# Weighted sums of a head pair gathered in one PSUM bank and read once, in the three attention stages of a two-block transformer

## The chip, the cores and the metric

One core of one Trainium2 chip runs the whole program; nothing is shared with other cores. The metric is the time of one execution on the device in microseconds (us). The engines are TensorE (PE, with its weight loads as PEld), VectorE (DVE), ScalarE (ACT), GpSimd (POOL) and SyncE (SP, which issues the transfers). Each works through its own list of instructions in order, and they meet only at semaphores. PSUM, which TensorE writes, has eight banks of 512 floats on each of the 128 partitions; they are numbered 0 to 7 below.

## The reference, cut to what matters

The input has 512 tokens of width 1024. Two blocks follow one another, each of two layers. Three of the layers hold attention with 16 heads of dimension 64, and these three are what the change touches:

```python
# first block, odd layer: keys chosen by top_k of an index score, bias by distance
logits = einsum('bqhd,bqkhd->bqhk', qb, ksel) * C_HEAD_DIM ** -0.5 + bias
probs  = softmax(where(valid, logits, -inf))
out    = einsum('bqhk,bqkhd->bqhd', probs, vsel)
return x + (out * silu(z)) @ w_out

# second block, layer 0: window of 128 keys, one sink per head
o = banded_attention(q, k, v, A_WINDOW, rel_table, sinks)
return o.reshape(B, S, ATTN_WIDTH) @ w_o + b_o

# second block, layer 1: three branches, each with its gate
o = gates[..., 0:1] * o_cmp + gates[..., 1:2] * o_slc + gates[..., 2:3] * o_win
return o.reshape(B, S, ATTN_WIDTH) @ w_o
```

The rest is dense projections, a chunkwise recurrence, pooling, norms and two feed-forward layers.

## The kernel before, in words

The program is a list of stages, and each stage hands every engine its own code. The order of the work on an engine is written out by hand in loops over steps; no scheduler moves anything.

Class `Attention` (line 1906) is used three times: for the odd layer of the first block (below: the first attention stage), for the windowed layer (the second) and for the two full branches of the last layer (the third; its compressed branch is computed before and lies in `oT`). The work is cut into steps `(m, t, e)`: `m` is one of 8 pairs of heads (128 features), `t` one of 4 query tiles of 128 queries, `e` the branch. In a pair, the tiles come in the order 3, 1, 2, 0, so the number of 128-key blocks in a causal step goes 4, 2, 3, 1. The first and second stage have 4 steps per pair (`per_pair`) and 32 in all (`NS`); the third has two branches, 8 steps per pair and 64 in all.

A step `s` goes through a pipeline:

- PE `score(s)`: the products of queries and keys into two of the banks 0 to 3 (L2002; in the first stage two matmuls with the mask stand ahead of some, L1999).
- DVE `logit(s)`: adds the bias, writes the logits to SBUF and keeps the row maximum (L2070). ACT `exp(s)` follows (L2164), then DVE `share` (the reciprocal of the row sum, L2076) and POOL `divide` (L2128).
- PE `turn(s)`: transposes of the probabilities, 2 per key block (L2016), into banks 4 and 5 for even steps or bank 6 for odd ones. DVE and ACT `keep(s)` copy them to SBUF (L2098, L2100, L2173).
- PE `mix(s)`: probabilities times values, 2 matmuls per key block (L2033), one for each head of the pair, into the upper or lower 64 partitions of a piece 128 columns wide, which method `O(s)` names.
- DVE `finish(s)`: reads that piece, 128 partitions x 128 columns, and adds it to `oT` (third stage, L2086), multiplies it into `zT` (first stage, L2088) or copies it to `oT` (second stage, L2090), and counts up `att_outs`.
- When the steps of a pair are done, ACT `split_high(m)` (L2177) and POOL `split_low(m)` (L2140) make the two parts of the pair's rows that the following projection multiplies.

Round `s` of the PE loop issues `score(s)`, `turn(s-3)`, `mix(s-5)`. Round `s` of the DVE loop issues `finish(s-6)`, `logit(s)`, `share(s-1)`, `keep(s-3)`. ACT's `split_high` stands in round 6 after the last step of a pair, POOL's `split_low` in round 7 after it.

Where a step can have more than two key blocks (first and third stage, flag `halves`), all pieces lie in columns 0 to 127 of bank 7, so each `mix` waits until the `finish` of the step before it has read them; only the last three steps alternate between banks 3 and 7. In the second stage the pieces alternate between banks 7 and 5, and a `mix` waits for the `finish` of the step two before it. After the last `score`, in round `NS`, the PE code also runs `lead_in`, the first products of the following projection (L298 to L300: 6 of the 8 blocks of its first tile, three matmuls each); after the last `mix` that projection goes on with its second tile.

Of the kernel before, what the change touches and what calls it, by code (L numbers as in the profile page):

```python
# [24 lines left out]
ALU = mybir.AluOpType  # L25
# [3 lines left out]
P = 128  # L29
SEQ = 512  # L30
DM = 1024
MT = DM // P
# [1873 lines left out]
class Attention(Stage):  # L1906
# [5 lines left out]
    def __init__(self, k, q, key, value, keys, n_bias, out, hi, lo, room, before=None, table=None, bias=None, add=False, times=None,  # L1912
                 mask=None, sink=None, gate=None, branches=1, bias_all=None, masked_bias=None, ready=None, finishing=None,
                 mask_made=None, turning=None, first_pe=None, first_act=None, trail_act=None, first_dve=None):


        self.k, self.q, self.key, self.value, self.keys, self.n_bias = k, q, key, value, keys, n_bias
        self.out, self.hi, self.lo, self.before, self.table, self.bias = out, hi, lo, before, table, bias
        self.add, self.times, self.mask, self.sink, self.gate = add, times, mask, sink, gate
        self.bias_all, self.masked_bias, self.ready_q, self.finishing, self.mask_made = bias_all, masked_bias, ready, finishing, mask_made  # L1920
        self.trail, self.trail_act = before is not None and before.trail is not None, trail_act
        self.turning, self.first_pe, self.first_act, self.following = turning, first_pe, first_act, None
        self.first_dve = first_dve
        self.pad = 0 if sink is None else 1
        self.pooled = (1, 2) if masked_bias is not None else ()
        self.steps = [(m, t, e) for m in range(MT) for e in range(branches) for t in (3, 1, 2, 0)]
        self.NS, self.per_pair = len(self.steps), 4 * branches
        probs_of, self.pT, self.st = room
        self.probs_of = [ap.rearrange("p (x n) -> p x n", x=2) for ap in probs_of]
        self.turned_of = [self.pT[:, 0:1024], self.pT[:, 1024:1536]]  # L1930
        self.T = [k.banks[:, 4:6, :].rearrange("p a b -> p (a b)"), k.banks[:, 6, :]]
        self.flip = 1 if before is not None and before.bank(before.last_in_turn()) < 2 else 0
        NS, sg = self.NS, k.sig
        self.landed = [sg(f"att_bias{i}").take(16 * (MT // 2) if bias is not None else 0) for i in range(2)]
        self.scores, self.logits = sg("att_scores").take(NS), sg("att_logits").take(2 * NS)
        self.probs, self.dens = sg("att_probs").take(2 * NS), sg("att_dens").take(NS)
        self.ready, self.turned, self.mixed = sg("att_ready").take(2 * NS), sg("att_turned").take(NS), sg("att_mixed").take(NS)
        self.kept = [sg(n).take(NS // 2) for n in ("att_kept_even", "att_kept_odd")]
        self.halves = len(keys(3)[2]) > 2
        self.rest = sg("att_kept_rest").take(NS // 2 if self.halves else 0)  # L1940
        self.outs = sg("att_outs").take(NS)
        self.added = sg("att_bias_masked").take(2 * MT if self.pooled else 0)
        self.high, self.low = sg("att_high").take(MT), sg("att_low").take(MT)

# [5 lines left out]

    def O(self, s):

        if not self.halves:
            return self.k.banks[:, 7 - 2 * (s % 2), 0:P]
        return self.k.banks[:, 3 if s in (self.NS - 3, self.NS - 1) else 7, 0:P]

    def with_mask(self, m, t):
        to = self.masked_bias[:, m % 2, 0:2, :] if t == 1 else self.masked_bias[:, m % 2, 2:5, :]
# [23 lines left out]
    def on_pe(self, pe):  # L1982
        nc, before, evac = self.k.nc, self.before, self.k.sig("tile_steps")
        steps, keys, S, T, kept = self.steps, self.keys, self.S, self.T, self.kept
# [36 lines left out]
        def mix(s):  # L2021
            m, t, e = steps[s]
            blocks = keys(t)[2]
            if s == self.NS - 3 and self.halves:
                pe.wait_ge(self.logits.sem, self.logits.at(2 * self.NS))
            pe.wait_ge(self.outs.sem, self.outs.at(s if s < self.NS - 3 and self.halves else s - 1))
            pe.wait_ge(kept[s % 2].sem, kept[s % 2].at(s // 2 + 1))
            if self.halves and s % 2 == 0:
                pe.wait_ge(self.rest.sem, self.rest.at(s // 2 + 1))
            last = len(blocks) - 1  # L2030
            for b, (kb, r) in enumerate(blocks):
                for x in range(2):
                    ins = nc.tensor.matmul(self.O(s)[64 * x:64 * x + 64, :], self.value(e, m, x, kb, r),  # L2033
                                           self.turned_of[s % 2][0:r, (2 * b + x) * P:(2 * b + x + 1) * P],
                                           start=(b == 0), stop=(b == last))
            ins.then_inc(self.mixed.sem, 1)

        for s in range(self.NS + self.MIX):
# [14 lines left out]
    def on_dve(self, dve):  # L2053
        nc, steps, keys, st, pad = self.k.nc, self.steps, self.keys, self.st, self.pad
# [20 lines left out]
            dve.wait_ge(self.probs.sem, self.probs.at((s + 1) * 2))  # L2075
            nc.vector.reciprocal(st[:, s % 4, 2, :], st[:, s % 4, 1, :]).then_inc(self.dens.sem, 1)  # L2076

        def finish(s):
            m, t, e = steps[s]
            r = slice(t * P, (t + 1) * P)  # L2080
            o = self.out(m)[:, r]
            dve.wait_ge(self.mixed.sem, self.mixed.at(s + 1))
            if self.finishing is not None and s % self.per_pair == 0:
                self.finishing(dve, m)
            if self.add:
                nc.vector.tensor_tensor(o, self.O(s), o, ALU.add).then_inc(self.outs.sem, 1)  # L2086
            elif self.times is not None:
                nc.vector.tensor_tensor(o, self.O(s), self.times(m)[:, r], ALU.mult).then_inc(self.outs.sem, 1)  # L2088
            else:
                nc.vector.tensor_copy(o, self.O(s)).then_inc(self.outs.sem, 1)  # L2090

        def keep(s):
            blocks = keys(steps[s][1])[2]
# [6 lines left out]
                nc.vector.tensor_copy(self.turned_of[0][0:r, 512:w], self.T[0][0:r, 512:w]).then_inc(self.rest.sem, 1)  # L2100

        for s in range(self.NS + self.FINISH):
            if 0 <= s - self.FINISH < self.NS:
                finish(s - self.FINISH)
            if s < self.NS:
                logit(s)
            if 0 <= s - 1 < self.NS and not (self.trail and s == 2):
                share(s - 1)
            if self.first_dve is not None and s < 2:
                self.first_dve(dve, s)  # L2110
            if self.trail and s == 1:
                share(1)
            if self.trail and s == 2:
                self.before.evict(dve, "dve", self.before.tiles - 1)
            if 0 <= s - self.TURN < self.NS and (self.halves or (s - self.TURN) % 2 == 1):
                keep(s - self.TURN)
# [39 lines left out]
    def on_act(self, act):  # L2156
# [16 lines left out]
            nc.scalar.activation(self.turned_of[0][0:r, 0:w], self.T[0][0:r, 0:w], ACT.Copy).then_inc(self.kept[0].sem, 1)  # L2173

        def split_high(m):
            act.wait_ge(self.outs.sem, self.outs.at(self.per_pair * (m + 1)))
            nc.scalar.activation(self.hi(m), self.out(m), ACT.Copy).then_inc(self.high.sem, 1)  # L2177

        for s in range(self.NS + self.HIGH):
# [967 lines left out]
```

## Time and profile before

| | |
|---|---|
| time, median of 3 runs | 1933.11 us (1933.01 to 1933.32) |
| profiled execution, first to last instruction | 1933.0 us |
| PE busy | 1910.9 us, 99% of the span |
| DVE busy | 1056.5 us, 55% |
| ACT busy | 769.1 us, 40% |
| POOL busy | 353.2 us, 18% |
| chain that ended last: share of PE | 90% |
| chain: share of DVE | 6% |

The span of the profile is 0.1 us from the median, so a sum made against the profiled execution can be set against the median as it stands. The chain is followed back from the last instruction, at each step to what released it. An engine's idle time ahead of an instruction is given with the instruction that ended it; where the profile says "issue", the engine waited for nothing that it shows. The ends of matmuls are modelled, and the starts are measured: how long a group of matmuls really took is read from its start to the start of the next group.

### The profile page before, as it was taken

To read this page: it belongs to the slowest core of one execution; us is meant where nothing else is said; L and a number is where in the kernel's file an instruction comes from. 1 tells how busy PE (TensorE), PEld (TensorE's weight loads), DVE (VectorE), ACT (ScalarE), POOL (GpSimd) and SP (SyncE) were. 2 spreads that over 40 slices of the span, in tenths; PEclk is the share of its full clock that TensorE was granted. 3 is DMA by queue.
4 is the path that set the end of the run, shared out by engine and by line. 5 is a ranking of instruction groups with operands and counts; after the bars stand their busy time and mean duration, and the time that the engine had idled before them with its cause. 6 is when DMAs were issued, how large, how long until landed. Compare 5 with 4: busy or idle time off the path is not lost.

```text
span 1933.0 us, 25271 instructions
## 1 busy us (share of the span) xinstructions
PE 1910.9 (99%) x9688; PEld 1508.1 (78%) x9688; DVE 1056.5 (55%) x2005; ACT 769.1 (40%) x1407; POOL 353.2 (18%) x443
## 2 busy tenths in 40 slices
PE   9999999999999999999999999999999999999998
PEld 7887778888777668768888888888766788888886
DVE  4567644444699755475544443343777555444323
ACT  4343434433354554474322222232566442222213
POOL 0640000001130761062000000040266310000002
PEclk9999999999999999999999999999999999999999
DMA  9452324442423223313333333365100133333232
GB/s 206 133 174 66 101 89 149 152 142 76 111 66 88 76 56 87 93 50 88 98 99 98 98 93 99 92 182 170 36 2 2 45 98 98 100 97 99 99 98 77
DMA packets 297246, 187.67 MB, mean 97 GB/s; under 512 B 32543, under 2 KB 274719, under 8 KB 296870
## 3 DMA queue, kind: packets, MB, share of 16 engines
q1 hardware_dynamic: 288958, 168.02, 30.7%
q10 hardware_dynamic: 8168, 18.03, 2.4%
q8 instruction: 78, 1.28, 0.3%
q14 instruction: 42, 0.34, 0.1%
HBM read 183.79 MB, written 17.96 MB: 104 GB/s over the span
## 4 chain that ended last, share of the span: by engine, by line
PE 90%; DVE 6%; ACT 2%; issue 1%; DMA 1%; POOL 0%; ACTq 0%; SPq 0%; DVEq 0%
PE banks L298 21%; PE banks L299 21%; PE banks L300 21%; PE banks L2033 4%; PE banks L2002 4%; PE banks L2016 4%; PE banks L600 2%; PE banks L598 2%; PE banks L599 2%; PE banks L412 2%; PE banks L414 2%; PE banks L413 2%; PE banks L950 1%; DVE idx_score L1216 1%; PE banks L958 1%
## 5 line engine op out<-in xcount | busy, mean ns | idle before, releaser
L2399 DVE TENSOR_TENSOR wlo<-raw,whi 128x1024 fp32r<-128x1024 f32 (+1 forms) x281 | 361.5, 1288 | 322.7 <-ACT whi L2390 322.2
L298 PE MATMUL banks<-xs,wlo 128*128 128x512 f32 x1336 | 533.0, 399 | 0.1
L300 PE MATMUL banks<-xs,whi 128*128 128x512 f32 x1336 | 521.5, 390 | 0.0
L299 PE MATMUL banks<-xs,whi 128*128 128x512 f32 x1336 | 521.4, 390 | 0.0
L2390 ACT ACTIVATE whi<-raw 128x1024 fp32r<-128x1024 f32 (+1 forms) x281 | 293.1, 1045 | 248.7 <-PE banks L300 100.6
L298 PEld LDWEIGHTS banks<-xs,wlo 128*128 128x128 f32 x1336 | 251.3, 188 | 60.6 <-issue 7.4
L299 PEld LDWEIGHTS banks<-xs,whi 128*128 128x128 f32 x1336 | 251.5, 188 | 53.8 <-issue 3.3
L300 PEld LDWEIGHTS banks<-xs,whi 128*128 128x128 f32 x1336 | 251.3, 188 | 53.2
L524 POOL TENSOR_TENSOR squares<-squares,x_tmp 128x512 f32<-128x512 f32 x35 | 46.9, 1341 | 685.3 <-ACT x_tmp L516 685.3
L2128 POOL TENSOR_SCALAR prob<-prob,long_stat,gt_s 128x512 f32<-128x512 f32 (+3 forms) x128 | 76.5, 607 | 125.1 <-DVE long_stat L2076 125.1
L2963 ACT ACTIVATE a_hi<-ff_tmp 128x512 fp32r<-128x512 f32 x44 | 27.8, 632 | 166.1 <-DVE ff_tmp L2962 166.1
L2960 ACT ACTIVATE ff_tmp<-ff_tmp 128x512 f32<-128x512 f32 x44 | 27.8, 632 | 165.7 <-DVE ff_tmp L2959 165.7
L2164 ACT ACTIVATE prob<-prob,long_stat 128x512 f32<-128x512 f32 (+3 forms) x128 | 70.6, 552 | 40.3 <-DVE long_stat L2070 39.9
L2424 ACT ACTIVATE xs<-hT,gains 128x512 fp32r<-128x512 f32 x40 | 29.0, 724 | 134.2 <-DVE hT L2419 111.0
L2016 PEld LDWEIGHTS banks<-ident,prob 128*128 128x128 f32 x432 | 45.8, 140 | 40.5 <-issue 36.2
L412 PE MATMUL banks<-wlo,xs 128*128 128x512 f32 x192 | 75.1, 391 | 0.3 <-DVE wlo L2399 0.3
L678 POOL TENSOR_TENSOR tok_scaled<-tok,last_gain 128x512 f32<-128x512 f32 x8 | 10.3, 1286 | 353.6 <-DVE tok L656 353.6
L413 PE MATMUL banks<-whi,xs 128*128 128x512 f32 x192 | 74.8, 389 | 0.0
L414 PE MATMUL banks<-whi,xs 128*128 128x512 f32 x192 | 74.8, 389 | 0.0
L2962 DVE TENSOR_TENSOR ff_tmp<-banks,ff_tmp 128x512 f32<-128x512 f32 x44 | 30.4, 691 | 78.0 <-PE banks L300 78.0
L2959 DVE TENSOR_TENSOR ff_tmp<-banks,row_scale 128x512 f32<-128x512 f32 x44 | 30.4, 691 | 75.9 <-PE banks L300 75.8
L2016 PE MATMUL banks<-ident,prob 128*128 128x128 f32 x432 | 68.0, 285 | 2.1 <-ACT pT L2173 1.0
(402 smaller groups left out, 3217.6 us busy)
## 6 DMA issues: line engine op xcount, KB each, us to landing
raw<-in_ffn_w_gu SPq DMA_DIRECT2D x88, 512.0 KB, 3.8
raw<-in_e_w_in SPq DMA_DIRECT2D x56, 512.0 KB, 3.9
raw<-in_ffn_w_down SPq DMA_DIRECT2D x38, 512.0 KB, 3.5
s_skew<-s_bias ACTq DMA_DIRECT2D x6, 2560.0 KB
raw<-in_o_w_in SPq DMA_DIRECT2D x21, 512.0 KB, 4.0
raw<-in_e_w_out SPq DMA_DIRECT2D x16, 512.0 KB, 3.9
raw<-in_b_w_in SPq DMA_DIRECT2D x15, 512.0 KB, 3.9
raw<-in_a_w_qkv SPq DMA_DIRECT2D x10, 512.0 KB, 4.0
```

The costliest lines, as they stand in the source:

```text
L298: nc.tensor.matmul(out, k.wlo[:, chunk.slot, at, :], self.x_hi(kt), start=first, stop=False)
L299: nc.tensor.matmul(out, k.whi[:, chunk.slot, at, :], self.x_lo(kt), start=False, stop=False)
L300: ins = nc.tensor.matmul(out, k.whi[:, chunk.slot, at, :], self.x_hi(kt), start=False, stop=last)
L412: nc.tensor.matmul(out, self.x_hi(kt)[:, r], rest[:, b, :], start=kt == 0, stop=False)
L413: nc.tensor.matmul(out, self.x_hi(kt)[:, r], high[:, b, :], start=False, stop=False)
L414: ins = nc.tensor.matmul(out, self.x_lo(kt)[:, r], high[:, b, :], start=False, stop=kt == MT - 1)
L2002: ins = nc.tensor.matmul(S(s, x)[:, 0:nk], self.q[r, m, t * P:(t + 1) * P], self.key(e, m, x)[r, k0:k0 + nk], start=not masked, stop=True)
L2016: ins = nc.tensor.transpose(T[s % 2][0:r, (2 * b + x) * P:(2 * b + x + 1) * P], self.probs_of[s % 4][:, x, self.pad + b * P:self.pad + b * ...
L2033: ins = nc.tensor.matmul(self.O(s)[64 * x:64 * x + 64, :], self.value(e, m, x, kb, r), self.turned_of[s % 2][0:r, (2 * b + x) * P:(2 * b + ...
L2128: nc.gpsimd.tensor_scalar(pr, pr, self.st[:, s % 4, 2, x:x + 1], g, ALU.mult, ALU.mult).then_inc(self.ready.sem, 1)
L2390: self.nc.scalar.activation(self.whi[:, chunk.slot, 0:chunk.blocks, :], self.raw[:, chunk.slot, 0:chunk.blocks, :], ACT.Copy).then_inc(sel ...
L2399: self.nc.vector.tensor_tensor(self.wlo[:, chunk.slot, 0:chunk.blocks, :], self.raw[:, chunk.slot, 0:chunk.blocks, :], hi.bitcast(F32), AL ...
```

## The change

`O(s)` now gives columns `128*t` to `128*t + 127` of one bank, named by the new method `sums(m)`: bank 7 for every pair in the first and third stage, and bank 7 or 5 by turns from pair to pair in the second. The four query tiles of a pair stand side by side in it; in the third stage the two branches of a tile are summed in the same columns.

Only the first `mix` of a pair carries `start=True` (on its first key block), and only it waits for `att_outs`: in the first and third stage for the `finish` of the pair before, in the second for that of the pair two before. All other mixes of a pair wait only for their transposed probabilities. `finish` is called with a pair and not with a step: once per pair, in round 6 after the pair's last step, it reads 128 partitions x 512 columns. ACT's `split_high` waits for a count of pairs. Bank 3 is no longer used by the last steps.

```diff
--- before.py
+++ after.py
@@ -1938,7 +1938,7 @@
         self.kept = [sg(n).take(NS // 2) for n in ("att_kept_even", "att_kept_odd")]
         self.halves = len(keys(3)[2]) > 2
         self.rest = sg("att_kept_rest").take(NS // 2 if self.halves else 0)
-        self.outs = sg("att_outs").take(NS)
+        self.outs = sg("att_outs").take(MT)
         self.added = sg("att_bias_masked").take(2 * MT if self.pooled else 0)
         self.high, self.low = sg("att_high").take(MT), sg("att_low").take(MT)
 
@@ -1950,9 +1950,11 @@
 
     def O(self, s):
 
-        if not self.halves:
-            return self.k.banks[:, 7 - 2 * (s % 2), 0:P]
-        return self.k.banks[:, 3 if s in (self.NS - 3, self.NS - 1) else 7, 0:P]
+        m, t, e = self.steps[s]
+        return self.sums(m)[:, t * P:(t + 1) * P]
+
+    def sums(self, m):
+        return self.k.banks[:, 7 if self.halves else 7 - 2 * (m % 2), :]
 
     def with_mask(self, m, t):
         to = self.masked_bias[:, m % 2, 0:2, :] if t == 1 else self.masked_bias[:, m % 2, 2:5, :]
@@ -2021,9 +2023,9 @@
         def mix(s):
             m, t, e = steps[s]
             blocks = keys(t)[2]
-            if s == self.NS - 3 and self.halves:
-                pe.wait_ge(self.logits.sem, self.logits.at(2 * self.NS))
-            pe.wait_ge(self.outs.sem, self.outs.at(s if s < self.NS - 3 and self.halves else s - 1))
+            opens = s % self.per_pair == 0
+            if opens:
+                pe.wait_ge(self.outs.sem, self.outs.at(m if self.halves else m - 1))
             pe.wait_ge(kept[s % 2].sem, kept[s % 2].at(s // 2 + 1))
             if self.halves and s % 2 == 0:
                 pe.wait_ge(self.rest.sem, self.rest.at(s // 2 + 1))
@@ -2032,7 +2034,7 @@
                 for x in range(2):
                     ins = nc.tensor.matmul(self.O(s)[64 * x:64 * x + 64, :], self.value(e, m, x, kb, r),
                                            self.turned_of[s % 2][0:r, (2 * b + x) * P:(2 * b + x + 1) * P],
-                                           start=(b == 0), stop=(b == last))
+                                           start=(opens and b == 0), stop=(b == last), skip_group_check=True)
             ins.then_inc(self.mixed.sem, 1)
 
         for s in range(self.NS + self.MIX):
@@ -2075,19 +2077,17 @@
             dve.wait_ge(self.probs.sem, self.probs.at((s + 1) * 2))
             nc.vector.reciprocal(st[:, s % 4, 2, :], st[:, s % 4, 1, :]).then_inc(self.dens.sem, 1)
 
-        def finish(s):
-            m, t, e = steps[s]
-            r = slice(t * P, (t + 1) * P)
-            o = self.out(m)[:, r]
-            dve.wait_ge(self.mixed.sem, self.mixed.at(s + 1))
-            if self.finishing is not None and s % self.per_pair == 0:
+        def finish(m):
+            o = self.out(m)
+            dve.wait_ge(self.mixed.sem, self.mixed.at(self.per_pair * (m + 1)))
+            if self.finishing is not None:
                 self.finishing(dve, m)
             if self.add:
-                nc.vector.tensor_tensor(o, self.O(s), o, ALU.add).then_inc(self.outs.sem, 1)
+                nc.vector.tensor_tensor(o, self.sums(m), o, ALU.add).then_inc(self.outs.sem, 1)
             elif self.times is not None:
-                nc.vector.tensor_tensor(o, self.O(s), self.times(m)[:, r], ALU.mult).then_inc(self.outs.sem, 1)
+                nc.vector.tensor_tensor(o, self.sums(m), self.times(m), ALU.mult).then_inc(self.outs.sem, 1)
             else:
-                nc.vector.tensor_copy(o, self.O(s)).then_inc(self.outs.sem, 1)
+                nc.vector.tensor_copy(o, self.sums(m)).then_inc(self.outs.sem, 1)
 
         def keep(s):
             blocks = keys(steps[s][1])[2]
@@ -2100,8 +2100,9 @@
                 nc.vector.tensor_copy(self.turned_of[0][0:r, 512:w], self.T[0][0:r, 512:w]).then_inc(self.rest.sem, 1)
 
         for s in range(self.NS + self.FINISH):
-            if 0 <= s - self.FINISH < self.NS:
-                finish(s - self.FINISH)
+            done = s - self.FINISH + 1
+            if done > 0 and done % self.per_pair == 0:
+                finish(done // self.per_pair - 1)
             if s < self.NS:
                 logit(s)
             if 0 <= s - 1 < self.NS and not (self.trail and s == 2):
@@ -2173,7 +2174,7 @@
             nc.scalar.activation(self.turned_of[0][0:r, 0:w], self.T[0][0:r, 0:w], ACT.Copy).then_inc(self.kept[0].sem, 1)
 
         def split_high(m):
-            act.wait_ge(self.outs.sem, self.outs.at(self.per_pair * (m + 1)))
+            act.wait_ge(self.outs.sem, self.outs.at(m + 1))
             nc.scalar.activation(self.hi(m), self.out(m), ACT.Copy).then_inc(self.high.sem, 1)
 
         for s in range(self.NS + self.HIGH):
```

What stands on DVE's queue in the third stage where the last step of a pair is finished, before the change. (`oT` holds the attention output, `long_stat` the row statistics, `prob` the probabilities, `pT` the transposed ones; ISA rows are the logits and the read of their maximum.)

```order
L2076 RECIPROCAL long_stat_250<-long_stat_250 128x2 [waits att_probs]
L2100 COPY pT_254<-banks 128x512 [waits att_turned,att_mixed]
L2086 TENSOR_TENSOR oT_185<-banks,oT_185 128x128 [waits att_mixed]
L2070 ISA prob_253,long_stat_250<-banks,bias_all_241 128x512 [waits att_scores,att_turned]
L2070 ISA long_stat_250 128x1
L2070 ISA prob_253,long_stat_250<-banks,bias_all_241 128x512
L2070 ISA long_stat_250 128x1
L2076 RECIPROCAL long_stat_250<-long_stat_250 128x2 [waits att_probs]
L2098 COPY pT_254<-banks 128x512 [waits att_turned,att_mixed]
L2086 TENSOR_TENSOR oT_185<-banks,oT_185 128x128 [waits att_mixed]
L2070 ISA prob_253,long_stat_250<-banks,bias_all_241 128x256 [waits att_scores,att_turned]
```

The same place after it:

```order
L2078 RECIPROCAL long_stat_250<-long_stat_250 128x2 [waits att_probs]
L2100 COPY pT_254<-banks 128x512 [waits att_turned,att_mixed]
L2072 ISA prob_253,long_stat_250<-banks,bias_all_241 128x512 [waits att_scores,att_turned]
L2072 ISA long_stat_250 128x1
L2072 ISA prob_253,long_stat_250<-banks,bias_all_241 128x512
L2072 ISA long_stat_250 128x1
L2078 RECIPROCAL long_stat_250<-long_stat_250 128x2 [waits att_probs]
L2098 COPY pT_254<-banks 128x512 [waits att_turned,att_mixed]
L2086 TENSOR_TENSOR oT_185<-banks,oT_185 128x512 [waits att_mixed]
L2072 ISA prob_253,long_stat_250<-banks,bias_all_241 128x256 [waits att_scores,att_turned]
```

The read ahead of the 512-wide logits is gone, and the one behind the `pT` copy of 512 has become four times as wide; everything queued behind it, the logits of the next step first, stands behind the wide read.

What stands on PE's queue in the third stage where the products of a new pair begin (`vt_s` are the values, `kT_s` and `qT_s` keys and queries), before:

```order
L2016 MATMUL banks<-ident_50,prob_253 128x128 [waits att_ready,att_kept_rest,att_kept_even]
L2016 MATMUL banks<-ident_50,prob_253 128x128 x5
L2033 MATMUL banks<-pT_254,vt_s_235 64x128 [waits att_kept_rest,att_kept_even,att_outs]
L2033 MATMUL banks<-pT_254,vt_s_235 64x128 x7
L2002 MATMUL banks<-kT_s_234,qT_s_233 128x384 [waits att_logits]
L2002 MATMUL banks<-kT_s_234,qT_s_233 128x384
L2016 MATMUL banks<-ident_50,prob_253 128x128 [waits att_ready,att_kept_odd]
L2016 MATMUL banks<-ident_50,prob_253 128x128
L2033 MATMUL banks<-pT_254,vt_s_235 64x128 [waits att_kept_odd,att_outs]
L2033 MATMUL banks<-pT_254,vt_s_235 64x128 x3
```

And after:

```order
L2018 MATMUL banks<-ident_50,prob_253 128x128 [waits att_ready,att_kept_rest,att_kept_even]
L2018 MATMUL banks<-ident_50,prob_253 128x128 x5
L2035 MATMUL banks<-pT_254,vt_s_235 64x128 [waits att_kept_rest,att_kept_even,att_outs]
L2035 MATMUL banks<-pT_254,vt_s_235 64x128 x7
L2004 MATMUL banks<-kT_s_234,qT_s_233 128x384 [waits att_logits]
L2004 MATMUL banks<-kT_s_234,qT_s_233 128x384
L2018 MATMUL banks<-ident_50,prob_253 128x128 [waits att_ready,att_kept_odd]
L2018 MATMUL banks<-ident_50,prob_253 128x128
L2035 MATMUL banks<-pT_254,vt_s_235 64x128 [waits att_kept_odd]
L2035 MATMUL banks<-pT_254,vt_s_235 64x128 x3
```

No matmul moves, and the opening one still waits for `att_outs`. In the changed program these are the only such waits that are left: 8 in each stage, one for each pair, where each of the 128 steps had one.

## Rows read from the trace of the kernel before

**Rows 1.** Attention stages: window, its length, busy us (instructions) by engine; then clock, DMA

```profile
634.00:720.00 86.00, 85.00 (x674) 54.92 (x673) 58.38 (x233) 55.33 (x158) 67.60 (x88) 1.00 0.19 50
806.00:875.00 69.00, 67.21 (x528) 44.42 (x527) 49.22 (x245) 48.27 (x157) 38.04 (x72) 1.00 0.15 40
1374.00:1525.00 151.00, 147.94 (x1312) 96.64 (x1312) 113.17 (x456) 99.76 (x303) 86.45 (x136) 1.00 0.02 5
```

**Rows 2.** Who PE's weight loads waited for: us in total, times, longest

```profile
PEld banks L2033 <- DVE oT L2086: 4.1, 16, 0.6
...
PEld banks L2033 <- DVE zT L2088: 2.6, 9, 0.6
PEld banks L2033 <- DVE oT L2090: 2.3, 12, 0.5
```

**Rows 3.** Timeline, third stage, a pair's end: start, us, engine, line

```profile
1437.75 0.67 DVE L2098 COPY pT<-banks 128x512 f32<-128x512 f32 x1
...
1437.81 0.87 PE L2016 MATMUL banks<-ident,prob 128*128 128x128 f32 x6
...
1438.33 0.28 DVE L2086 TENSOR_TENSOR oT<-banks,oT 128x128 f32<-128x128 f32 x1
...
1438.67 1.09 PE L2033 MATMUL banks<-pT,vt_s 128*64 128x128 f32 x16
...
1439.69 0.92 PE L2002 MATMUL banks<-kT_s,qT_s 64*128 64x384 f32 x4
```

**Rows 4.** DVE groups by shape: times, busy us, mean ns, idle before

```profile
L2419 DVE TENSOR_TENSOR hT<-banks,hT 128x512 f32<-128x512 f32 x32 | 22.1, 689 | 44.0 <-PE banks L300 44.0
L2098 DVE COPY pT<-banks 128x512 f32<-128x512 f32 x32 | 21.5, 672 | 0.9 <-PE banks L2033 0.9
...
L2086 DVE TENSOR_TENSOR oT<-banks,oT 128x128 f32<-128x128 f32 x64 | 18.0, 281 | 0.2 <-PE banks L2033 0.2
```

**Rows 5.** PE timeline, first stage: transposes and products of the first pair

```profile
646.76 0.88 PE L2016 MATMUL banks<-ident,prob 128*128 128x128 f32 x6
647.57 1.09 PE L2033 MATMUL banks<-pT,vt 128*64 128x128 f32 x16
```

**Rows 6.** The same place of a later pair in the first stage

```profile
674.53 0.88 PE L2016 MATMUL banks<-ident,prob 128*128 128x128 f32 x6
...
675.09 0.28 DVE L2088 TENSOR_TENSOR zT<-banks,zT 128x128 f32<-128x128 f32 x1
...
675.42 1.09 PE L2033 MATMUL banks<-pT,vt 128*64 128x128 f32 x16
```

**Rows 7.** Timeline, second stage, a pair's end and two rounds on

```profile
839.98 0.66 PE L2016 MATMUL banks<-ident,prob 128*128 128x128 f32 x4
840.16 0.28 DVE L2090 COPY oT<-banks 128x128 f32<-128x128 f32 x1
...
840.56 0.66 PE L2033 MATMUL banks<-pT,vt_w 128*64 128x128 f32 x8
...
841.50 0.93 POOL L2128 TENSOR_SCALAR win_prob<-win_prob,win_stat 128x256 f32<-128x256 f32 x2 [0.45 <-DVE win_stat L2076]
...
843.16 0.66 PE L2016 MATMUL banks<-ident,win_prob 128*128 128x128 f32 x4
```

**Rows 8.** Timeline, third stage, last rounds, with idle time and its releaser

```profile
1512.47 0.66 PE L2016 MATMUL banks<-ident,prob 128*128 128x128 f32 x4
...
1513.53 0.44 PE L2033 MATMUL banks<-pT,vt_s 128*64 128x128 f32 x4 [0.40 <-DVE oT L2086]
...
1520.98 0.42 DVE L2098 COPY pT<-banks 128x256 f32<-128x256 f32 x1 [0.33 <-PE banks L2033]
...
1521.65 0.20 PEld L2033 LDWEIGHTS banks<-pT,vt_s 128*64 128x64 f32 x4 [0.30 <-DVE oT L2086]
```

**Rows 9.** After the third stage: the last pair's low part, and its first use

```profile
1523.18 1.29 POOL L2140 TENSOR_TENSOR long_lo<-oT,long_hi 128x512 fp32r<-128x512 f32 x1 [7.60 <-ACT long_hi L2177]
...
1526.91 0.39 PE L298 MATMUL banks<-long_hi,wlo 128*128 128x512 f32 x1
```

## The prediction, made before the changed kernel was run

> **What bounds the kernel now.** I began with the page's list of engines: PE is busy for 99% of the span and makes 90% of the chain that ended last, so a change counts only by what it does to PE's own queue. Then the three attention stages one by one, by windows [rows 1]: PE is busy for 85.00 of 86 us, 67.21 of 69 and 147.94 of 151, at the full granted clock (1.00), while DVE is busy for 58.38, 49.22 and 113.17. DVE, whose work the change cuts, has room in all three stages; a DVE microsecond is worth something only where PE waits for it. So the third view is the list of what PE's weight loads waited for, at the products that the change touches (L2033) [rows 2]: 16 times for the adds into `oT`, 9 times for `zT`, 12 times for the copies. These sums are small, 4.1, 2.6 and 2.3 us, and part of each is the ordinary gap of a change from one kind of matmul to the next, so the starts of the groups have to be compared in the timeline.
>
> In the third stage at the end of a pair [rows 3]: DVE copies transposed probabilities (1437.75), then reads the products of the pair's last tile (1438.33, 0.28 us, so until 1438.61), and the products of the next pair start at 1438.67, 0.06 us after that end. The six transposes ahead of them began at 1437.81, so 0.86 us pass. Where nothing is waited for, the same six transposes take 0.81 us until the products start [rows 5]. So PE already waits here, by 0.05 us: the read sets the start. In the first stage the same place shows 0.89 us, a wait of 0.08, and again the products begin 0.05 us behind the read (675.09 + 0.28 = 675.37, start at 675.42) [rows 6]. At the other three steps of a round of four I find no such wait. In the second stage the four transposes take 0.58 us until the products [rows 7], as elsewhere in that stage: no wait.
>
> **What is removed.** Of the small reads 128 go: 32, 32 and 64. At 281 ns each [rows 4] they are 36 us of DVE time, and 24 wide reads at 689 come in for 16.5: DVE saves about 19 us, most of it where it has idle time anyway. On PE three things go.
>
> - In the third stage the wait between the two branches of a pair. There are 7 such places in the steady rounds (the eighth stands in the tail), 0.05 us each [rows 3, 5]: 0.35 us.
> - Round 64 of the third stage, where a step's products come right behind four transposes with no scores between: 1513.53 - 1512.47 = 1.06 us, against 0.58 for four transposes without a wait [rows 7, 8]. The step opens no pair, so its wait goes: 0.48 us. The first stage has the same code and the same longest wait of 0.6 us at the weight loads [rows 2]: 0.96 us for both. The second, with two banks, has none here.
> - The last step of each stage. Its weight loads started at 1521.65 behind a read. They still need the copy of their own probabilities, which ends at 1520.98 + 0.42 = 1521.40, so they can start at about 1521.45 [rows 8]: 0.20 us. The same for the other two stages, which I did not work out apart: 0.60 us.
>
> **What is added.** The wide read. The nearest row is the same kind of operation, a PSUM bank plus an SBUF tile over 128 x 512: 689 ns against 281 for the small one, 0.41 us more; a plain copy of 512 columns takes 672 [rows 4]. It stands where the small read of the pair's last step stood, with the same 0.67 us copy ahead of it, and that copy stands behind 512-wide logits which wait for PE. So it starts no earlier, although the reads before it are gone, and it ends 0.41 us later. In the first and third stage all pairs share bank 7, and the next pair's first products wait for exactly this read: they start 0.41 us later, at 1439.08 instead of 1438.67 in the pair shown. Nothing absorbs this: PE's queue behind the waiting products is `score`, `turn` and `mix` of the next rounds, which start one behind another. Queued behind the read on DVE are the next logits, late by the same 0.41 us, which ACT, POOL and then PE meet shifted alike.
>
> How often: the third stage has 8 pairs, of which 7 find a pair before them: 7 places. The first stage too, but its last pair opens in round 33, behind the 18 products that `lead_in` puts into round 32, which are some microseconds of PE's time; the read is over by then. So 6 there. In the third stage the last pair opens in round 61, in steady work. 13 x 0.41 = 5.33 us.
>
> In the second stage an opener waits for the pair two before, whose read stands a whole pair earlier. The wide copy still holds up DVE by 672 - 281 = 0.39 us, and behind it the logits of the next step and the reciprocal of the one before. The nearest reader is POOL's division, done at 841.50 + 0.93 = 842.43, for transposes that PE starts at 843.16 [rows 7]. The slack is 0.73 us; 0.34 would be left. Cost nothing, and if that cover fails it is the slower rival below.
>
> After the last product of a stage the wide read ends 0.41 - 0.20 = 0.21 us later than now, measured from PE's own work, and so do ACT's high part and POOL's low part. The low part ends at 1523.18 + 1.29 = 1524.47 and is first used in the neighbourhood of 1526.91 [rows 9]: over 2 us of slack, cost nothing.
>
> **Sum.** 5.33 - 0.35 - 0.96 - 0.60 = +3.4 us. The profiled execution spans 1933.0 us and the median is 1933.11, so the sum is added as it is: 1936.5 us. Bounds of the terms: below, the opener costs 0.39 (the copy's row) and the last step gives 0.30, the whole idle time shown for it: 5.07 - 0.35 - 0.96 - 0.90 = +2.9. Above, an opener could cost more than the difference of two reads: in round 64 PE itself idles 0.40 us and the start is 0.48 late [rows 8], so 0.08 may be lost in starting again: 13 x 0.49 = 6.37, and with nothing gained at the last step +5.1. The likeliest case's own range is 1936.0 to 1938.2.
>
> **The rivals.** About 0.2%, 3.9 us, is what a measurement here can tell from no change, so the line to "slower" runs at 1937.0, inside that range.
>
> - The wide read is not what the opener waits for, because DVE, freed of the small reads, arrives earlier. Then only the gains are left, -1.9 us: 1931.2. For it: four or eight reads less per pair. Against it: the last copy and read hang on logits that hang on PE's scores, and the small read already sets the opener's start by 0.05 to 0.08 us. 6%.
> - DVE is what holds the stages, and fewer instructions pay. From the rows: 19 us less of DVE time, all of it on the path, gives 1914. Against it: DVE has 20 to 38 us of idle time in each stage [rows 1], and PE's starts follow one another. [...] 4%.
> - Slower: the second stage loses its cover. The delay of 0.39 us in each of 7 pairs reaches PE's transposes by way of DVE's reciprocal and POOL's division. The point from which it decides is a delay above the 0.73 us of slack; ACT's copies of the same rounds come later too and could add up to it. Price at most 7 x 0.39 = 2.7 us on top: 1939.2. For it: in this stage DVE's delay is not shared by PE, so it isn't carried along. 12%.
> - Left for what I don't see: 5%.
>
> **How the numbers follow.** The forecast has 73%: 1936.5. About three tenths of it lies above 1937.0, since the upper bound of an opener is further off than the lower: 22% slower, 51% within. With the slower rival's 12%, slower is 34%. Within 0.2% are 51%, the first rival's 6% (1931.2) and the 5% unseen: 62%. Faster: 4%. The range runs from 1931.0, to take in the first rival, to 1939.0, just short of the slower rival's full price. Left out are the 4% of the DVE rival and parts of the last two.
>
> **What would show it.** In the profile of the changed kernel: 24 wide reads of about 0.69 us, and none of 128 columns. In the third stage, at every second group of 16 product matmuls, about 1.27 us from the six transposes to the products, and 0.81 at the others; in the first stage 1.30 at six places. The third stage longer by about 7 x 0.41 - 0.35 - 0.48 - 0.20 = 1.8 us, the first by 6 x 0.41 - 0.48 - 0.20 = 1.8, the second shorter by 0.2. Busy DVE time down by some 19 us with nothing to show for it. The prediction is wrong if the openers' distance stays at 0.86, if PE shows new waits at L2016 or at scores, or if the second stage grows.

## The result, and the profile after

The changed kernel takes 1938.21 us (median of 9 runs, 1938.05 to 1938.38), the kernel before 1933.20 on the same chip (9 runs): 5.0 us more, a ratio of 1.0025 with a 95% interval of 1.0016 to 1.0035. It is slower, since the interval leaves out 1. Whether it is slower by more than the 3.9 us (0.2%) that the prediction gave as the line is open: the interval has 1.0020 inside it. The forecast was 1936.5 us, 1.7 less than measured, and the range of 1931.0 to 1939.0 holds the result.

DVE reads 24 times 512 columns, as said, and has lost the small reads. The groups by shape (times, busy us, mean ns, idle before), to set beside [rows 4]:

```profile
L2086 DVE TENSOR_TENSOR oT<-banks,oT 128x512 f32<-128x512 f32 x8 | 5.5, 682 | 0.5 <-PE banks L2035 0.5
L2088 DVE TENSOR_TENSOR zT<-banks,zT 128x512 f32<-128x512 f32 x8 | 5.5, 682 | 0.5 <-PE banks L2035 0.5
L2090 DVE COPY oT<-banks 128x512 f32<-128x512 f32 x8 | 5.4, 678 | 0.5 <-PE banks L2035 0.5
```

What PE's weight loads waited for at the lines of the change (us in total, times, longest; products are now L2035, transposes L2018), against [rows 2]:

```profile
PEld banks L2018 <- ACT pT L2174: 4.6, 8, 1.4
PEld banks L2035 <- DVE oT L2086: 4.4, 7, 0.6
PEld banks L2035 <- DVE zT L2088: 3.9, 6, 0.7
```

Seven and six waits for a read are left, and they are longer. They are one for each opener (the first products of a pair) in the steady rounds, those before the last rounds of a stage, its tail. The first row is new in size: before, PE's loads met that copy of ACT twice, for 2.2 us.

```profile
PEld banks L2016 <- ACT pT L2173: 2.2, 2, 1.4
```

The third stage at a pair's end, PE's own rows, beside [rows 3]:

```profile
1439.94 0.87 PE L2018 MATMUL banks<-ident,prob 128*128 128x128 f32 x6
1441.21 1.09 PE L2035 MATMUL banks<-pT,vt_s 128*64 128x128 f32 x16 [0.39 <-DVE oT L2086]
1442.23 0.92 PE L2004 MATMUL banks<-kT_s,qT_s 64*128 64x384 f32 x4
```

and DVE's at the same place:

```profile
1439.88 0.67 DVE L2098 COPY pT<-banks 128x512 f32<-128x512 f32 x1
1440.47 0.68 DVE L2086 TENSOR_TENSOR oT<-banks,oT 128x512 f32<-128x512 f32 x1
1441.07 0.41 DVE L2072 CUSTOM_DVE_ANT_0 prob<-banks,bias_all 128x256 f32<-128x256 f32 x1
```

From the transposes to the products it is 1441.21 - 1439.94 = 1.27 us, where it was 0.86. The read starts 0.59 us behind the start of the copy (1439.88 to 1440.47), as before (1437.75 to 1438.33, 0.58 us), though the copy is recorded as 0.67 us long; the records of neighbouring operations on DVE overlap by 0.08 us here. The read ends at 1440.47 + 0.68 = 1441.15, and the products start 0.06 us after that. The scores behind them follow after 1442.23 - 1441.21 = 1.02 us, as before (1438.67 to 1439.69), so the delay is passed on whole.

Starts are measured, so a stage can be measured from PE's first scores to the first product of the following projection behind the last `mix`. All runs below are measured this way (us; a stage's length is from the one profiled execution of the kernel, and a second profile of the kernel before agrees within 0.06; the times are medians, and the kernel before ran beside each at 1933.1 to 1933.2):

| kernel | first stage | second | third | sum | time |
|---|---|---|---|---|---|
| before | 81.51 | 64.32 | 146.04 | 291.87 | 1933.20 |
| changed | 83.24 | 65.81 | 147.78 | 296.83 | 1938.21 |
| `stage2_old` | 83.24 | 64.30 | 147.79 | 295.33 | 1936.69 |
| `act_first` | 83.24 | 64.21 | 147.79 | 295.24 | 1936.58 |
| `read256` | 81.63 | 65.84 | 145.92 | 293.39 | 1935.07 |
| `read128` | 80.83 | 65.80 | 144.97 | 291.60 | 1932.86 |
| `two_reads` | 80.84 | 64.08 | 144.99 | 289.91 | 1931.41 |
| `small_sooner` | 80.97 | 64.26 | 145.22 | 290.45 | 1931.68 |
| `early_read` | 80.32 | 64.17 | 144.57 | 289.06 | 1930.46 |

The three stages lose 1.73, 1.49 and 1.74 us, together 4.96, which is the whole difference of the times. The profiled spans do not show this: 1933.0 before and 1936.3 after are only 3.3 apart. The windows of the start of the program say why. Before (length, then busy times, then the granted clock, the last number but two, as a share of full speed):

```profile
25.00:30.00 5.00, 4.90 (x15) 3.24 (x14) 4.86 (x6) 2.45 (x4) 0.00 (x0) 0.69 0.66 62
```

In the changed kernel the same window has a granted clock of 1.00 and 21 matmuls in place of 15. The profiled execution of the kernel before had a short stretch at half the clock, long ahead of the attention stages: from 27 to 30 us the granted clock is 0.50 there and 1.00 in the changed kernel, and the same kind of product started every 0.43 us against 0.23. The stretch cost 1.7 us: the first scores start at 636.39 there and at 634.69 in the changed kernel. Most executions of the same kernel don't have it: in the last experiment six of ten have a span 1.7 to 2.0 us shorter than the profiled one.

### The profile page after: what moved, and what is told of

Read it like the earlier page. It is cut to its first block, busy times and chain, and to the rows that moved or that the text cites. A ratio compares the mean times of both kernels' runs of the same rounds, so it can differ in the third digit from the quotient of the medians.

```text
span 1936.3 us, 25095 instructions
## 1 busy us (share of the span) xinstructions
PE 1908.2 (99%) x9688; PEld 1505.6 (78%) x9688; DVE 1045.9 (54%) x1901; ACT 768.2 (40%) x1407; POOL 353.4 (18%) x443
## 4 chain that ended last, share of the span: by engine, by line
PE 87%; DVE 7%; ACT 2%; issue 2%; DMA 1%; POOL 0%; ACTq 0%; DVEq 0%; SPq 0%
PE banks L298 21%; PE banks L300 20%; PE banks L299 20%; PE banks L2035 4%; PE banks L2004 3%; PE banks L2018 3%; PE banks L598 2%; PE banks L599 2%; PE banks L600 2%; PE banks L412 2%; PE banks L413 2%; PE banks L414 2%; PE banks L950 1%; DVE idx_score L1216 1%; PE banks L958 1%
## 5 line engine op out<-in xcount | busy, mean ns | idle before, releaser
L2018 PEld LDWEIGHTS banks<-ident,prob 128*128 128x128 f32 x432 | 45.8, 141 | 40.6 <-issue 36.2
L2018 PE MATMUL banks<-ident,prob 128*128 128x128 f32 x432 | 68.0, 284 | 2.1 <-ACT pT L2174 1.0
```

Source lines behind the costliest of these rows:

```text
L2018: ins = nc.tensor.transpose(T[s % 2][0:r, (2 * b + x) * P:(2 * b + x + 1) * P], self.probs_of[s % 4][:, x, self.pad + b * P:self.pad + b * ...
```

## The experiments

**The second stage as it was.** In the changed kernel the second stage alone gets its small reads and its two alternating pieces back:

```diff
     def O(self, s):
         m, t, e = self.steps[s]
+        if not self.halves:
+            return self.k.banks[:, 7 - 2 * (s % 2), 0:P]
         return self.sums(m)[:, t * P:(t + 1) * P]
...
-            if done > 0 and done % self.per_pair == 0:
+            if done > 0 and not self.halves:
+                finish_step(done - 1)
+            elif done > 0 and done % self.per_pair == 0:
                 finish(done // self.per_pair - 1)
```

> The changed kernel, with the second (windowed) stage as it was before: one read per step, banks 7 and 5 by turns. Theory A (three separate costs: 7 and 6 openers at 0.41 us in the third and first stage, less what their tails give, and in the second stage ACT's late copy of the transposed probabilities, 0.27 us in each of 7 pairs): the second stage is back at 64.3 us from its first scores to the first product of the following projection (before 64.32, changed 65.81), the other two stay at 83.2 and 147.8; time 1936.7 us. Theory B (the second stage grew because the first handed it over in another state): it stays near 65.8 us and the time near 1938.2.

Measured: 1936.69 us, the second stage 64.30 and the others unmoved at 83.24 and 147.79. So the growth of the second stage comes from the change in that stage and not from how the first hands over, and the costs add up.

**Through which engine the second stage waits.** Only the order of two calls on ACT is changed, in the second stage and in one round of four:

```diff
+            early = not self.halves and s % 4 == 1 and self.TURN < s < self.NS
+            if early:
+                keep(s - self.TURN)
             if s < self.NS:
                 exp(s)
```

> The changed kernel with one thing turned round in the second stage: in the rounds in which DVE reads a whole pair, ACT copies the transposed probabilities (L2174) before it takes the exponentials of that round's logits, instead of after. Nothing on DVE or POOL changes. Theory A (PE's new wait before the transposes comes through ACT's queue, where the copy stands behind exponentials that the wide read made late): the 0.69 us from scores to transposes go back to 0.42, the second stage takes 64.1 us, the time is 1936.5 us. Theory B (the wait comes through DVE's reciprocal and POOL's division, as the prediction's rival had it): no change, 65.8 us and 1938.2 us.

Measured: 1936.58 us, the second stage 64.21, 1.6 us less than in the changed kernel and 0.1 above theory A's 64.1. In the changed kernel's trace, ACT and PE in that round and the next (every second row of ACT, the read of a sum, is left out):

```profile
849.36 0.51 ACT L2165 ACTIVATE win_prob<-win_prob,win_stat 128x257 f32<-128x257 f32 x1 [1.05 <-DVE win_stat L2072]
849.87 0.49 ACT L2165 ACTIVATE win_prob<-win_prob,win_stat 128x257 f32<-128x257 f32 x1
850.30 0.49 PE L2004 MATMUL banks<-kT_w,qT_w 64*128 64x128 f32 x4
850.36 0.57 ACT L2174 ACTIVATE pT<-banks 128x512 f32<-128x512 f32 x1
850.99 0.66 PE L2018 MATMUL banks<-ident,win_prob 128*128 128x128 f32 x4 [0.19 <-ACT pT L2174]
```

ACT waits for late logits (1.05 us idle), its two exponentials push the copy of the transposed probabilities to 850.36, and PE, which transposes the next even step into the same bank, gets there at 850.99: 0.69 us behind the scores instead of 0.42. With ACT's calls the other way round, the same place is

```profile
849.57 0.49 PE L2004 MATMUL banks<-kT_w,qT_w 64*128 64x128 f32 x4
...
850.00 0.66 PE L2018 MATMUL banks<-ident,win_prob 128*128 128x128 f32 x4
```

0.43 us and no wait, with DVE's read as wide as in the changed kernel, and POOL's division of that round as late against PE's scores (0.42 us behind them, 0.45 in the changed kernel). So the route is the copy on ACT's queue and not POOL's division. Of the six places of this kind four are back at 0.42 us and two stand at 0.46 and 0.48; what holds those, 0.1 us in all, no run shows.

**The price by the width of the read.** The first and third stage read only part of a pair's columns; the sums of the other tiles are left out. The second stage stays as changed.

```diff
+            r = slice(0, 256 if self.halves else 4 * P)
-            o = self.out(m)
+            o = self.out(m)[:, r]
...
-                nc.vector.tensor_tensor(o, self.sums(m), o, ALU.add).then_inc(self.outs.sem, 1)
+                nc.vector.tensor_tensor(o, self.sums(m)[:, r], o, ALU.add).then_inc(self.outs.sem, 1)
```

> The changed kernel with the read of a pair in the first and third stage cut to 256 of its 512 columns; the sums of the other two query tiles are left out of the output. Theory A (an opener waits for the whole of the read, so its price goes with the width): each of the 13 openers costs 0.14 us over the small read instead of 0.41, since 256 columns take about 0.42 us; the first stage takes 83.24 - 6 x 0.27 = 81.6 us and the third 147.78 - 7 x 0.27 = 145.9, the second stays at 65.8; time 1934.7 us. Theory B (what costs is that PE stops and starts again, not how long): the openers' distance stays near 1.27 us and the time near 1938.2.

Measured: 1935.07 us, stages of 81.63 and 145.92. The rows of this run's reads and of PE at a pair's end:

```profile
L2087 DVE TENSOR_TENSOR oT<-banks,oT 128x256 f32<-128x256 f32 x8 | 3.3, 416 | 0.5 <-PE banks L2035 0.5
```

```profile
1439.46 0.87 PE L2018 MATMUL banks<-ident,prob 128*128 128x128 f32 x6
1440.46 1.09 PE L2035 MATMUL banks<-pT,vt_s 128*64 128x128 f32 x16
```

1.00 us from transposes to products, 0.14 over the 0.86 of before; the read takes 416 ns, 135 more than 281. The profiled execution had the slow stretch at the start of the program (a granted clock of 0.67 from 25 to 30 us) and took 1936.28 us; three more took 1936.18 to 1936.26, and the median of the other seven is 1934.85 us (1934.65 to 1935.17), nearer to the 1934.7 of theory A.

The same edit with 128 in place of 256:

> As read256, with 128 of the 512 columns read in the first and third stage; three query tiles' sums are left out of the output. Theory A: each opener costs what it did in the kernel before (0.86 us from the six transposes in the third stage, 0.89 in the first); stages of 80.8, 65.8 and 145.0 us, time 1933.1 us. With read256 and the changed kernel this gives three widths on one line, 0.137 us per 128 columns and opener. Rival: a flat part, if a floor of the waiting itself is there: above 81.2 and 145.5.

Measured: 1932.86 us, stages of 80.83 and 144.97. From 128 to 256 to 512 columns the first stage takes 80.83, 81.63 and 83.24 us, so 0.133 and 0.134 us per opener and 128 columns (six openers); the third 144.97, 145.92 and 147.78, so 0.136 and 0.133 (seven). The added cost is a straight line in the width, which refutes theory B. The three widths can't show a part that is the same for all, since PE waits at all three of them. Such a part is small, though: at each width the products of the third stage start 0.06 us behind the read's end, and with 128 columns the whole distance is 0.86 us, only 0.05 above the 0.81 of an opener that waits for nothing.

**The read in two parts.** Nothing is left out; the last products of a pair wait for the first part, so the part's read and the writes of those products into the bank take turns. What would happen without that wait, no run shows.

```diff
-            if done > 0 and done % self.per_pair == 0:
-                finish(done // self.per_pair - 1)
+            if done >= 0:
+                m, at = divmod(done, self.per_pair)
+                if at == self.per_pair - 2 and self.parts(m) == 2:
+                    finish(m, slice(P, 4 * P), done)
+                if at == self.per_pair - 1:
+                    finish(m, slice(0, P if self.parts(m) == 2 else 4 * P), done)
```

> The changed kernel with the read of a pair in two parts wherever the next pair opens in steady rounds: tiles 1 to 3 (384 columns) one round earlier, where DVE stood idle ahead of its logits, and tile 0 (128 columns) where the wide read stood; the last products of a pair wait for the first part. Everything is computed. Theory A: openers start where they did before the change, the gains stay (0.35 us between branches, 0.48 us in the tails of the first and third stage, 0.20 us at the last step of each), and ACT's copy in the second stage is not late: stages of 80.8, 64.1 and 145.0 us, time 1931.3 us, 1.9 us under the kernel before. Rival: the 384-column read (0.56 us) does not fit into the gap of 0.5 us ahead of the 512-wide logits, or holds up the pair's last products; then 0.1 to 0.3 us come back per pair in 20 places, and the time is 1933 to 1937 us.

Measured: 1931.41 us, a ratio of 0.9992 (0.9983 to 1.0001) to the kernel before; stages of 80.84, 64.08 and 144.99 against the expected 80.8, 64.1 and 145.0. The interval of the ratio holds 1, so the times alone don't show a gain; the stages' lengths do, 1.96 us less in sum than before. The gains of the change are there, once the opener's wait is not lengthened.

**The wide read one place earlier.** DVE's copy of transposed probabilities (L2098) stood ahead of the read, although the products for the read were ready: in the changed kernel PE's last ones end at 1438.94 + 0.44 = 1439.38, and the read starts at 1440.47. The second stage has ACT's order from `act_first`.

```diff
-            if done > 0 and done % self.per_pair == 0:
+            if done > 0 and done % self.per_pair == 0 and not self.halves:
                 finish(done // self.per_pair - 1)
...
+            if self.halves and done >= 0 and (done + 1) % self.per_pair == 0:
+                finish((done + 1) // self.per_pair - 1)
             if 0 <= s - self.TURN < self.NS and (self.halves or (s - self.TURN) % 2 == 1):
                 keep(s - self.TURN)
```

> The changed kernel with the wide read of the first and third stage put one place earlier on DVE's queue, ahead of the copy of transposed probabilities that stood before it (L2098); in the second stage ACT's copy stands ahead of its exponentials as in the run act_first. Everything is computed. Theory A (an opener waits because the read stands behind that copy; DVE has the products of the pair's last tile by then): the read ends about 0.2 us before PE gets to the opener, so all openers start unhindered, 0.81 us after the six transposes, also the 0.05 to 0.08 us of the kernel before are gone. First stage 81.5 - 0.48 - 0.20 - 6 x 0.08 = 80.35 us, second 64.2, third 146.04 - 14 x 0.05 - 0.48 - 0.20 = 144.65; time 1930.6 us, 0.8 under two_reads. Rival: the next logits come 0.41 us late on DVE while PE no longer shares the delay, and a new wait shows at PE's transposes or scores, as in the second stage of the changed kernel; then 0.1 to 0.3 us per pair come back and the time is 1932 to 1934 us.

Measured: 1930.46 us, a ratio of 0.9988 (0.9979 to 0.9996); stages of 80.32, 64.17 and 144.57. The third stage at a pair's end:

```profile
1434.37 0.67 DVE L2086 TENSOR_TENSOR oT<-banks,oT 128x512 f32<-128x512 f32 x1
1434.43 0.88 PE L2018 MATMUL banks<-ident,prob 128*128 128x128 f32 x6
...
1434.96 0.68 DVE L2098 COPY pT<-banks 128x512 f32<-128x512 f32 x1
...
1435.24 1.09 PE L2035 MATMUL banks<-pT,vt_s 128*64 128x128 f32 x16
```

0.81 us from transposes to products, the distance of [rows 5] where nothing is waited for. The read is as wide as in the changed kernel, and ends at 1435.04, 0.20 us before PE's products start at 1435.24. The new waits of the rival did not come. This is the fastest version: 2.7 us under the kernel before, 7.8 under the changed one.

**The place of the read without the gathering.** The kernel before, with tile 0's small read ahead of the same copy:

```diff
+        def sooner(s):
+            return self.halves and 0 <= s < self.NS - 5 and s % 4 == 3
...
+            if sooner(s - self.FINISH + 1):
+                finish(s - self.FINISH + 1)
             if 0 <= s - self.TURN < self.NS and (self.halves or (s - self.TURN) % 2 == 1):
                 keep(s - self.TURN)
```

> The kernel before, with one 128-column read of every four (tile 0's) put ahead of that same copy on DVE's queue in the first and third stage; nothing is gathered. This asks how much of a gain needs the gathering at all. Theory A: only the 0.05 us of 14 places and the 0.08 us of 6 go; stages of 81.0, 64.3 and 145.3 us, time 1932.0 us. Rival (all of the gain of early_read is the place of the read): 1930.6 us.

Measured: 1931.68 us, a ratio of 0.9992 (0.9983 to 1.0001); stages of 80.97, 64.26 and 145.22. So of the 2.8 us by which `early_read` shortens the three stages, 1.4 come with the place of the read alone. The other 1.4 came only with the gathering. About 1 us of them is round 64 of the third stage and its like in the first: here the products still start 1.06 and 1.07 us behind four transposes, in `early_read` 0.58 and 0.59. Whether small reads put elsewhere in the tails would give that too was not tried.

**The kernel before once more.**

> The kernel before, unchanged, once more. Its profiled execution spans 1933.0 us although changed and other kernels spend about 1.8 us outside their span. Theory A (that one execution ran slower than the timed ones, through a stretch at half the granted clock near 27 to 30 us): a profile without such a stretch spans about 1931.4 us, with the same stage lengths 81.5, 64.3 and 146.0. Theory B (the kernel before really spends nothing outside its span): 1933.0 again.

Measured: 1933.19 us, stages of 81.49, 64.26 and 146.06. The profiled execution happened to have the slow stretch again: the granted clock of 25 to 30 us is 0.66. Its span was 1933.1 us and its own time 1934.91: 1.8 us lie outside the span, as in the changed kernel (1936.3 and 1938.05). That refutes theory B. The spans of the other nine executions are on record too: six span 1931.1 to 1931.4 us at times of 1932.94 to 1933.19, as theory A has it, and three span 1932.8 at 1934.6, like the profiled one. No stage lengths are known for these nine.

## Why the prediction was right, and where it was not

**Openers, 13 x 0.41 us: right.** 0.86 became 1.27 us in the third stage, in the first it was 1.29 or 1.30 where 0.89 stood. The three widths show that the price over the small read goes by the length of the read, and the seventh opener of the first stage did not wait, as said: 0.75 us from transposes to products before and after.

**Gains, 0.35 + 0.96 + 0.60 us: right.** `read128`, where openers cost what they did before, shows them alone: 81.51 - 80.83 = 0.68 us in the first stage (0.48 + 0.20 were forecast) and 146.04 - 144.97 = 1.07 in the third (0.35 + 0.48 + 0.20 = 1.03). The first and third stage came out at +1.73 and +1.74 for the forecast +1.8 each.

**The second stage, "cost nothing": wrong, and it is the whole miss.** Forecast was -0.2 us, measured +1.49: without the 1.7 between them the time is close to the forecast's. The step that failed was to name one reader of the late logits, POOL's division with 0.73 us of slack, as the nearest. Nearer was ACT's copy of the even steps' transposed probabilities: not fed by the late logits, but queued behind their exponentials. In the kernel before, the place shown above for the changed one is

```profile
849.11 0.57 ACT L2173 ACTIVATE pT<-banks 128x512 f32<-128x512 f32 x1
...
849.74 0.66 PE L2016 MATMUL banks<-ident,win_prob 128*128 128x128 f32 x4
```

The copy ended 0.06 us before PE's transposes, and in the changed kernel too the transposes start 0.05 or 0.06 us behind its end: there was no slack left. So it is in three of the six places of this kind; in the other three the copy ended 0.20 to 0.22 us ahead, and the delay used that up. Scores to transposes grew from 0.42 to 0.68 or 0.69 us in five places and from 0.44 to 0.83 in one, 1.7 us in all, less 0.2 at the last step. (The expectations say seven pairs; the trace shows six.) The slower rival had the stage, the shared cause and the upper price (2.7 us) right, and mentioned ACT's copies in half a sentence, but gave the route as DVE and POOL, the deciding point as 0.73 us, and 12%. Two of the signs that the prediction named for being wrong came: new waits at the transposes, and a second stage that grew. That the result still lies inside the range is owed to room that was left for other reasons: an opener costlier than its read, and most of this rival's full price. The mechanism of the second stage was missed.

**The span against the median: misread.** I took the 0.1 us between 1933.0 and 1933.11 as what lies around the span. It was a coincidence of 1.8 us outside the span and 1.7 us of slow clock inside it. The sum was a difference between starts in the attention stages, so nothing in it changed, but reading the two spans as the result would have given 3.3 us, near the forecast's 3.4, and hidden the second stage's loss.

**Rivals.** That the opener would not wait: no, 1.27 us. That DVE's instruction count holds the stages: no. DVE has dropped from 1056.5 to 1045.9 busy us and the kernel is slower. The forecast of 19 us less was itself off: the busy time fell by 10.6, probably since durations overlap on DVE: the small read at 1438.33 took 0.28 us, but the next operation started 0.20 us after its start, and behind the wide one at 1440.47, of 0.68 us, 0.60 us after it. With these distances the estimate is 128 x 0.20 - 24 x 0.60 = 11.2 us. It priced only that rival.

## What to carry to other kernels

Gathering small reads into a wide one saved time on the reading engine here (DVE is busy for 1045.9 us instead of 1056.5) and lengthened the one wait at which the buffer changes hands (1.27 us from transposes to products instead of 0.86); with a single buffer the price was the difference of two read lengths, 0.41 us, at each of 13 changes, and it went to nothing (0.81 us) when the read was put ahead of a copy that no engine was waiting for yet. When an operation gets longer, look at everything queued behind it and then at everything queued behind those on the next engines: the copy that stalled PE here (0.69 us from scores to transposes instead of 0.42) did not depend on the late data. And compare stages by the starts of the same instructions, not spans, before explaining a few microseconds.

## What the runs showed of the hardware

Where PE's opener waited for DVE's read of PSUM, of 128, 256 or 512 columns, each 128 columns more cost it 0.133 to 0.136 us. In the third stage the products started 0.06 us behind the read's end at every width, and the next group behind them kept its 1.02 us (1.03 with 256 columns), so a fixed part for stopping and starting is not above that 0.06 there. PE's idle gaps of 0.39 us ahead of the openers did not change the granted clock (1.00 in all three stages of the changed kernel). A stretch at half clock (0.50 from 27 to 30 us), in some executions of the same kernel, cost 1.7 us of the whole in the kernel before; PE's starts from 20.6 to 26.7 us, ahead of it, agree within 0.1 us with those of the changed kernel, which did not have it. What sets it off stays open.
